# Where the low parts of expert_u are made during a top-16 search: GpSimd from SBUF in place of VectorE from PSUM

## The reference, cut to what matters

```python
q = (xt @ w_pq).reshape(n_tok, 8, 2, 128)
scores = einsum('thcd,hckd->thck', q, sub_keys)      # 256 tokens, 16 sets of 128 scores
s_top, i_top = top_k(scores, 16)                     # for both halves of each of 8 heads
cand = s_top[:, :, 0, :, None] + s_top[:, :, 1, None, :]
best, pos = top_k(cand.reshape(n_tok, 8, 256), 16)
expert_idx = take_along_axis(cand_idx, pos)          # cand_idx = i_top[0]*128 + i_top[1]
gate = softmax(best)
act = gelu(einsum('thkd,td->thk', expert_u[expert_idx], xt))
out = einsum('thk,thkd->td', gate * act, expert_v[expert_idx])
```

## Time and profile before

| | |
|---|---|
| Median of three runs | 2268.61 us (2268.48 to 2272.78) |
| The profiled execution | 2266.69 us |
| its span | 2264.9 us |
| granted TensorE clock, mean | 0.976 |
| busy: PE, DVE, ACT, POOL | 93%, 72%, 49%, 12% of the span |
| first product with expert_u | 616.72 us from the span's start |
| part A | about 617 to 1044 us |
| pairs 26 to 63 | about 1044 to 1540 us |
| products with expert_v, last norm | about 1540 to 2265 us |

### The profile page before, as it was taken

One profiled execution on the slowest core, in us unless ns is written; L12 is line 12 of the kernel. 1 busy time (PEld: TensorE's weight loads), 2 busy tenths in 40 slices (PEclk: granted clock), 3 DMA queues, 4 the chain that ended last, 5 costly groups with the idle time before them and its releaser, 6 DMA issues.

```text
span 2264.9 us, 42561 instructions
## 1 busy us (share of the span) xinstructions
PE 2104.1 (93%) x12326; PEld 1860.0 (82%) x12326; DVE 1631.0 (72%) x2645; ACT 1108.1 (49%) x1888; POOL 270.6 (12%) x171
## 2 busy tenths in 40 slices
PE   8998898979878778889999999999999999999995
PEld 7887786768777777879999999998788888888884
DVE  4556656665588888989999999996555555555556
ACT  4554454445422222334666666655455555555552
POOL 0003301000100000002444444410000000000001
PEclk9999998989999999999999999999999999999998
DMA  7764452647444444545555555566865565555552
GB/s 231 221 207 144 142 169 82 209 144 205 135 125 119 122 112 124 144 139 164 161 157 158 159 157 157 159 174 200 225 202 191 193 193 194 193 192 192 193 194 103
DMA packets 253812, 378.42 MB, mean 167 GB/s; under 512 B 41809, under 2 KB 173009, under 8 KB 253137
## 3 DMA queue, kind: packets, MB, share of 16 engines
q1 hardware_dynamic: 253776, 377.98, 55.7%
HBM read 373.69 MB, written 4.19 MB: 167 GB/s over the span
## 4 chain that ended last, share of the span: by engine, by line
PE 51%; DVE 13%; issue 7%; DVEq 1%; SPq 0%; DMA 0%; ACT 0%; POOL 0%; ACTq 0%
PE ps L406 16%; PE ps L407 16%; PE ps L408 16%; DVE split_lo L1229 5%; PE ps L650 3%; DVE ps L1240 1%; DVE onehot L1397 0%; DVE onehot L1392 0%; DVE head_i L1299 0%; DVE pick_n L1402 0%; SPq L383 0%; DMA raw<-in_expert_v 0%; DVE head_p L1319 0%; DVE head_i L1307 0%; DVE head_p L1316 0%
## 5 line engine op out<-in xcount | busy, mean ns | idle before, releaser
L972 DVE TENSOR_TENSOR split_lo<-raw,split_hi 128x512 fp32r<-128x512 f32 x864 | 623.6, 725 | 519.6 <-ACT split_hi L717 519.4
L717 ACT ACTIVATE split_hi<-raw 128x512 fp32r<-128x512 f32 x864 | 544.4, 631 | 605.8 <-PE ps L408 588.7
L406 PE MATMUL ps<-act_hi,split_hi 128*128 128x256 f32 x2048 | 607.9, 297 | 82.5 <-DVE split_lo L1229 81.6
L407 PE MATMUL ps<-act_lo,split_hi 128*128 128x256 f32 x2048 | 586.5, 286 | 0.0
L408 PE MATMUL ps<-act_hi,split_lo 128*128 128x256 f32 x2048 | 586.0, 286 | 0.0
L876 ACT ACTIVATE split_hi<-ps 128x512 fp32r<-128x512 f32 x512 | 292.6, 594 | 465.3 <-DVE ps L1240 252.6
L406 PEld LDWEIGHTS ps<-act_hi,split_hi 128*128 128x128 f32 x2048 | 399.3, 195 | 107.2 <-DVE split_lo L1229 105.7
L406 PE MATMUL ps<-split_hi,whalf_hi 128*128 128x512 f32 x1024 | 398.7, 389 | 3.2 <-DVE split_lo L972 3.2
L407 PEld LDWEIGHTS ps<-act_lo,split_hi 128*128 128x128 f32 x2048 | 400.6, 196 | 0.0
L408 PEld LDWEIGHTS ps<-act_hi,split_lo 128*128 128x128 f32 x2048 | 399.5, 195 | 0.0
L407 PE MATMUL ps<-split_lo,whalf_hi 128*128 128x512 f32 x1024 | 398.4, 389 | 0.0
(11 more groups left out here) (172 smaller groups left out, 1448.8 us busy)
## 6 DMA issues: line engine op xcount, KB each, us to landing
raw<-in_expert_u SPq DMA_DIRECT2D x1024, 128.0 KB, 2.9
raw<-in_expert_v SPq DMA_DIRECT2D x256, 512.0 KB, 4.6
raw<-in_w_in SPq DMA_DIRECT2D x112, 512.0 KB, 3.8
raw<-in_w_out SPq DMA_DIRECT2D x32, 512.0 KB, 4.1
raw<-in_w_pq SPq DMA_DIRECT2D x128, 128.0 KB, 2.8
cst<-in_tables SPq DMA_DIRECT2D x4, 576.0 KB, 5.1
x_nat<-in_x SPq DMA_DIRECT2D x4, 512.0 KB, 6.9
x_dram<-x_cols SPq DMA_DIRECT2D x1, 2048.0 KB, 7.9
```

The lines of the kernel that those rows point to most:

```text
L406: nc.tensor.matmul(acc, l_hi, r_hi, start=first, stop=False)
L407: nc.tensor.matmul(acc, l_hi, r_lo, start=False, stop=False)
L717: nc.scalar.activation(split_hi[:, q % SPLITS, :], raw[:, q // 2, q % 2, :], ACT.Copy).then_inc(hi_ready, 1)
L972: vec.tensor_tensor(split_lo[:, q % SPLITS, :], raw[:, q // 2, q % 2, :], split_hi[:, q % SPLITS, :].bitcast(f32), ALU.subtract).then_inc( ...
```

## The change

For pairs 0 to 25 the transposes write to a new SBUF buffer, `u_cols` (four halves, 16 KB a partition), in place of PSUM. ScalarE rounds from `u_cols`. GpSimd makes all eight low parts of each of these pairs (208 in all), as a subtraction with both operands and the result in SBUF. VectorE keeps the transposes and the search, in a new order in which a transpose stands between an instruction and the one that needs it. ScalarE copies each set's scores to `head_s` (two buffers now) and keeps the results of each search (three copies), two sets behind and ahead. ScalarE rounds the first four units between the last score evictions, and the first transposes no longer wait for the evictions. The second fill of ones becomes two. From pair 26 on everything is as before. The core of the diff (definitions of buffers, and the removal of the parameters `own`, `part_a`, `nxt`, `next_a`, which had one value each, are left out):

```diff
+        u_cols = at("u_cols", [RAWS, 2, COLS], f32, W0 + 57344)
...
             def split_u(pair, q, part_a):
+                act.wait_ge(dve_turned, turned_at(q // 2, pair))
                 act.wait_ge(split_free, pair * 8 + (Q_U + q + 1))
-                nc.scalar.activation(split_hi[:, q % SPLITS, :], ps[:, 4 + q % 4, :], ACT.Copy).then_inc(hi_ready, 1)
+                src = u_cols[:, q // 2, q % 2, :] if part_a else ps[:, 4 + q % 4, :]
+                nc.scalar.activation(split_hi[:, q % SPLITS, :], src, ACT.Copy).then_inc(hi_ready, 1)
+            def stage_set(n, s):
+                if not isinstance(n, int):
+                    act.wait_ge(ranked, n - 1)
+                nc.scalar.activation(head_s[:, s, :, :], sc3[:, bass.ds(n * 2, 2), :], ACT.Copy
+                                     ).then_inc(set_staged, 1)
+            def keep_set(n, s):
+                act.wait_ge(ranked, n + 1)
+                nc.scalar.activation(idx_f[:, bass.ds(n, 1), :, :].rearrange("p a c k -> p (a c) k"), head_i[:, s, :, :],
+                                     ACT.Copy)
+                nc.scalar.activation(best[:, bass.ds(n, 1), :].rearrange("p a k -> p (a k)"), head_b[:, s, :], ACT.Copy)
+                nc.scalar.activation(pos_u[:, bass.ds(n, 1), :].rearrange("p a k -> p (a k)"), head_p[:, s, :],
+                                     ACT.Copy).then_inc(set_kept, 1)
...
                 for q in range(4, 8):
                     split_u(pair, q, part_a)
                 gelu(pair, 0, 0 in late_tiles)
+                if kept is not None:
+                    keep_set(*kept)
+                if staged_set is not None:
+                    stage_set(*staged_set)
                 split_u(pair + 1, 0, next_a)
...
+            for f in range(8):
+                act.wait_ge(sc_ready, f + 1)
+                nc.scalar.activation(scores[:, f // 4, f % 4 * 4:f % 4 * 4 + 4, :].rearrange("p s k -> p (s k)"),
+                                     ps[:, 2 + f % 2, :], ACT.Copy).then_inc(sc_out, 1)
+                if f == 1:
+                    act.wait_ge(sc_out, 1)
+                    for s in range(2):
+                        stage_set(s, s)
+                if f >= 4:
+                    split_u(0, f - 4, True)
+            u_pair(0, True, True)
+            with act.Fori(0, PH - 1) as i:
+                u_pair(i * 2 + 1, True, True, kept=(i * 2, 0), staged_set=(i * 2 + 2, 0))
+                u_pair(i * 2 + 2, True, True, kept=(i * 2 + 1, 1), staged_set=(i * 2 + 3, 1))
+            u_pair(SOFT - 1, True, True, kept=(SOFT - 2, 0))
+            u_pair(SOFT, True, True, kept=(SOFT - 1, 1))
...
+            def turn_u(pair, k, part_a=False):
+                dve.wait_ge(raw_ready[k], pair * DMA4 + (U_RAW + DMA4))
+                if part_a:
+                    if not (isinstance(pair, int) and pair == 0):
+                        dve.wait_ge(lo_ready, pair * 8 + (Q_U + 2 * k - 6))
+                    dst = u_cols[:, k, :, :]
...
+            def rank_set(lc, n, s):
+                dve.wait_ge(set_staged, n + 1)
+                dve.sem_inc(carried, 1)
+                dve.wait_ge(set_kept, n + 1)
+                dve.sem_inc(carried, 1)
+                turn_u(n + 1, 0, True)
+                top = [lc.add(vec.max(top_v[:, c, 0:8], cols[c])) for c in range(2)]
+                left = []
+                for c in range(2):
+                    lc.until(top[c])
+                    lc.add(vec.max_index(head_i[:, s, c, 0:8], top_v[:, c, 0:8], cols[c]))
+                    left.append(lc.add(vec.match_replace(half_rest[c], top_v[:, c, 0:8], cols[c], LOWEST)))
+                low = []
+                for c in range(2):
+                    lc.until(left[c])
+                    low.append(lc.add(vec.max(top_v[:, c, 8:16], half_rest[c])))
+                turn_u(n + 1, 1, True)
+                lc.until(low[1])
+                sums = lc.add(vec.tensor_tensor(cand[:, :, :], ...))
+                for c in range(2):
+                    lc.add(vec.max_index(head_i[:, s, c, 8:16], top_v[:, c, 8:16], half_rest[c]))
+                lc.until(sums)
+                first = lc.add(vec.max(head_b[:, s, 0:8], pairs))
+                turn_u(n + 1, 2, True)
+                lc.until(first)
+                lc.add(vec.max_index(head_p[:, s, 0:8], head_b[:, s, 0:8], pairs))
+                rest_of = lc.add(vec.match_replace(rest[:, :], head_b[:, s, 0:8], pairs, LOWEST))
+                lc.until(rest_of)
+                second = lc.add(vec.max(head_b[:, s, 8:16], rest[:, :]))
+                turn_u(n + 1, 3, True)
+                lc.until(second)
+                vec.max_index(head_p[:, s, 8:16], head_b[:, s, 8:16], rest[:, :]).then_inc(ranked, 1)
...
+                compared = [compare(h) for h in range(2)]
+                turn_u(pair, 0, True)
+                lc.until(compared[1])
+                selected = [select(h) for h in range(2)]
+                turn_u(pair, 1, True)
+                lc.until(selected[1])
+                collected = [collect(h) for h in range(2)]
+                turn_u(pair, 2, True)
+                turn_u(pair, 3, True)
+                lc.until(collected[1])
...
+                    def split_lo_u(pair, q):
+                        pool.wait_ge(hi_ready, pair * 8 + (Q_U + q + 1))
+                        eng.tensor_tensor(split_lo[:, q % SPLITS, :], u_cols[:, q // 2, q % 2, :],
+                                          split_hi[:, q % SPLITS, :].bitcast(f32), ALU.subtract).then_inc(lo_ready, 1)
+                    for q in range(8):
+                        split_lo_u(0, q)
                     pool.wait_ge(x1_out, 16)
                     pool.wait_ge(sc_ready, 8)
-                    top = 96
-                    eng.memset(wexp[:, LATE:top, :], 1.0).then_inc(ones_ready, 1)
+                    free_rows, kept_rows = 56, 88
+                    eng.memset(wexp[:, LATE:free_rows, :], 1.0).then_inc(ones_ready, 1)
+                    with pool.Fori(1, PAIRS_A) as i:
+                        for q in range(8):
+                            split_lo_u(i, q)
+                    pool.wait_ge(lo_ready, Q_U + 8 * PAIRS_A)
+                    eng.memset(wexp[:, free_rows:kept_rows, :], 1.0)
                     pool.wait_ge(topk_done, 1)
-                    eng.memset(wexp[:, top:NT, :], 1.0).then_inc(ones_ready, 1)
+                    eng.memset(wexp[:, kept_rows:NT, :], 1.0).then_inc(ones_ready, 1)
```

More of the change, by code:

```diff
@@ L244, in fill_place, with turned_at @@
             return f // 2 % 2, (f // 4 * 2 + f % 2) * 4
[L246 to L261, removed]
         PQ_RAW = Q_PQ // 8 * DMA1
         U_RAW = PQ_RAW + (Q_U - Q_PQ) // 8 * DMA4
-        V_RAW = [U_RAW + PAIRS_A * (DMA4 if k in DVE_A else DMA1)
-                 + (PAIRS - PAIRS_A) * (DMA4 if k in DVE_B else DMA1) for k in range(RAWS)]
+        V_RAW = U_RAW + PAIRS * DMA4
+        def turned_at(half, pair):
+            return pair * RAWS + (half + 1)
         block = ctx.enter_context(nc.Block())
@@ L614, in _, with score_pair @@
                 last.then_inc(sc_ready, 1)
-            def score_pair(pair, own, part_a, nxt=None, next_a=False, after=None):
+            def score_pair(pair, after=None):
                 for q in range(8):
@@ L1264, in add, with until @@
                     instruction.then_inc(v_chain, 1)
-                def step(self, instruction):
-                    self.add(instruction)
-                    dve.wait_ge(v_chain, self.i * self.steps + (self.first + self.n))
+                    return self.n
+                def until(self, n):
+                    dve.wait_ge(v_chain, self.i * self.steps + (self.first + n))
                     dve.sem_inc(carried, 1)
@@ L1333, in late_tile @@
+            with dve.Fori(0, PH) as i:
+                lc = LoopChain(i, c0, TOP_STEPS)
+                for s in range(2):
+                    rank_set(lc, i * 2 + s, s)
+                assert lc.n == TOP_STEPS, lc.n
+            chain.n += PH * TOP_STEPS
             def late_tile(pair, t):
@@ L1346, in apply_gates, with u_pair @@
                                   ).then_inc(gates_free, 1)
-            def u_pair(pair, own, part_a, nxt, next_a, late_tiles=False, groups=None, between=None):
+            def u_pair(pair, groups=None, between=None):
                 for k in (2, 3):
-                    split_turn(pair, k, own, part_a, nxt, next_a)
-                    if late_tiles and k == 2:
-                        if groups is not None and not isinstance(groups, int):
+                    split_turn(pair, k)
+                    if k == 2:
+                        if groups is not None:
                             dve.wait_ge(gates_free, groups + 2)
@@ L1358, in u_pair @@
                 for k in (4, 5):
-                    split_turn(pair, k, own, part_a, nxt, next_a)
-                    if late_tiles and k == 4:
+                    split_turn(pair, k)
+                    if k == 4:
                         if groups is not None:
```

(10 more changed lines are left out.)

193 lines of the change are left out of this document (65 added, 128 removed).

## The result

The changed kernel takes 2141.32 us (median of four runs, 2139.91 to 2144.47); the kernel before took 2268.55 beside it. The ratio is 0.9428, 95% interval 0.9415 to 0.9441. The forecast was 2141 us, 2134 to 2188. A second set of runs of the same file, `after_again`, the baseline of the experiments, gave 2140.72 us (five runs, 2140.44 to 2142.16), ratio 0.9431 (0.9417 to 0.9444).

What follows compares the result with a forecast made beforehand. VectorE's program order bounded part A, then TensorE would: start 613.8 plus 300.9 us gives 914.7 against 1044.1, 129.4 less, minus 2 for jams; 2266.69 - 127.4 = 2139.3, median 1.9 higher: 2141 us, range 2134 to 2188.

Steps and rivals of the forecast that it cites:

- TensorE the bound of part A, full clock, pitch 0.12: Pairs 0 to 25: TensorE always busy at full clock, 0.12 us a matmul, 11.52 us a pair; chance 62%.
- GpSimd's low part, 1.08 us: Each of GpSimd's 208 subtractions of 128x512 was to take 1.08 us, 8.6 us a pair against 11.52.
- The numbering on GpSimd, 11.0 of 11.52: In a numbering pair GpSimd needs 8.6 us for low parts plus 2.4 held by VectorE, 11.0 of TensorE's 11.52.
- second rival: GpSimd becomes the bound at 1.75 us a low part, 14.0 a pair: 64 us lost, 2205 us; chance 11%.
- The shared way into SBUF: VectorE's two-input instructions wait for GpSimd's running one: `cand` 0.4 us, four a numbering pair 0.7 each, holding GpSimd 0.6.
- Pair 16 on VectorE, about 7 us: In pair 16 VectorE has four transposes and the start of the softmax, about 7 us against 11.5, winning slack back.
- VectorE, a search, 10.9: VectorE's work in one search falls from 17.56 us to 10.9 (10.3 to 11.6), or 11.3 with port waits.
- first rival: VectorE stays the bound, 13.0 us a search and 14.2 a numbering: 33 us lost, 2174 us; chance 18%.
- ScalarE: ScalarE's added staging and keeping copies bring it to at most 7.4 of 11.52 us a search, costed at nothing.
- The start: Part A's first product comes at 613.8 us against 616.72, 2.9 us earlier, from 0 to 3.7.
- The end of part A: Two GpSimd fills of ones, 15.6 us, stay hidden behind pairs 25 and 26 by 1 us or more.
- The sum: Whole forecast: 26 pairs at 11.52, 1.4 for slow matmuls, earlier start, 2 us for jams: 127.4 us saved.

Runs made afterwards that it cites:

- pool_kinds: Changed kernel plus six GpSimd subtractions and products of 128x512 alone at its very start, with two full operands or one repeated; 2146.59 us (single run).
- exposed: Changed kernel with VectorE waiting for its own result before its transposes, not behind them, at three places of a search; 2140.55 us, ratio 0.9423.

## Why the prediction was right, point by point

- **TensorE the bound of part A, full clock, pitch 0.12:** as forecast. Measured to the same point as before (0.6 us ahead of the gelu, 1044.1 there and 921.5 here), part A took 921.5 - 618.73 = 302.8 us; the prediction had 300.9 and 2 for jams.
- **GpSimd's low part, 1.08 us: wrong,** 1.30 alone and 1.37 as the mean of all 208. The step that failed is "1.75 is about 1.1 plus one 0.6 of VectorE, so I take 1.08": all the rows of 1.04 to 1.12 had a repeated operand, which I had noted and then not priced, and `pool_kinds` puts the second full operand at 0.22. The row of 1.75 was read wrongly with it: like the low parts that meet VectorE (1.74 to 1.79) it fits 1.3 and a hold of 0.46, not 1.1 and 0.6. A row with two full operands was in the trace before, the 2.56 us for 1024 columns shown under `pool_kinds`; it gives 1.28. The Trainium skill's factor of about two (GPSIMD Engine Reference, "When to use GPSIMD") gave an estimate of 1.38, and I set it aside because of those rows; it was the nearer of the two (1.30 / 0.68 = 1.9). What saved the sum is the room: 281 us of work in 299.9 rather than 249 in 299.5.
- **The numbering on GpSimd, 11.0 of 11.52: wrong in both terms,** which partly cancel. Back to back, low parts that meet nothing start 1.26 us apart (a little less than they last, as they overlap), so eight are 10.1; the iteration is 11.93, so each of the four two-input instructions of VectorE holds GpSimd for (11.93 - 10.1) / 4 = 0.46, not 0.6. It ends 0.4 over TensorE's pace. Eight times that is 3.3, and TensorE lost 2.8 in 797 to 914 us. The second rival was therefore true for eight pairs of 26, at a price of 3 us instead of 15.
- **The shared way into SBUF:** right in kind, small in the sum. `cand` takes 0.38 when free and 1.04 to 1.52 when it waits, 0.54 on the mean: 0.16 of wait where I took 0.4. The comparisons and products wait 0.64 and 0.40 on the mean (1.325 and 1.076 against 0.68) where I took 0.7; singly they take 0.64 to 0.97 or 1.45 to 1.79. Transposes take 1.19 to 1.25 beside a busy GpSimd, and sums 0.65. The Trainium skill's rule (SBUF — State Buffer, "Who interferes with whom"), that VectorE instructions with one SBUF input go free outside the two-port modes and those with two do not, agrees with all of these.
- **Pair 16 on VectorE, about 7 us: a missed term.** I gave the softmax's start (a copy, a subtraction of two operands, two operations with a constant and a conversion) no wait, though the earlier trace rows shows a copy that waited. All five waited, two of them here:

```profile
814.33 1.38 DVE L1371 TENSOR_SCALAR pos_i<-pos_u 128x256 uint32<-128x256 uint32 x1
...
817.09 1.48 DVE L1373 CAST pos_f<-pos_i 128x512 f32<-128x512 uint32 x1
```

  In the kernel before, with GpSimd idle, these two took 0.29 and 0.43 us. The start of the softmax took 6.2 us (812.4 to 818.6), so with four transposes 10.9. That is still under 11.52.
- **VectorE, a search, 10.9:** lower. One period, with the row's wait taken off:

```profile
631.24 1.25 DVE L1249 STREAM_TRANSPOSE u_cols<-raw 128x1024 f32<-128x1024 f32 x1 [1.21 <-POOL split_lo L1575]
...
641.47 1.25 DVE L1249 STREAM_TRANSPOSE u_cols<-raw 128x1024 f32<-128x1024 f32 x1
```

  Work without a wait for GpSimd takes 641.47 - 631.24 = 10.23 us, its `cand` of 1.06 included, under the lower end of my 10.3 to 11.6 plus port wait. The order hid nearly all the stalls, and `exposed` shows that it need not have. The first rival (VectorE the bound, 18%) was 1.3 us a search away, and in the numbering VectorE was idle 1.27 us an iteration (10.66 us of work where I took 12.2); two more two-input instructions were enough to bring it about.
- **ScalarE:** costed at nothing, and that held; staging and keeping took 0.20 to 0.41 each, behind no wait.
- **The start:** 2.9 us forecast, 3.7 measured (16.19 from `q_t` to the first product before, 12.53 after), and the allowance of 1.4 for slow matmuls was not needed, as TensorE came without a gap.
- **The end of part A:** as forecast. The fills took 15.6 us (6.94 and 8.65) and ended 4.3 us before GpSimd's next work had its input:

```profile
917.97 6.94 POOL L1588 MEMSET wexp<- 128x8192 f32 x1
924.85 8.65 POOL L1590 MEMSET wexp<- 128x10240 f32 x1
937.76 3.76 POOL L1597 TENSOR_TENSOR hot<-small,picks_t 128x1024 f32<-128x1024 f32 x2 [4.26 <-DVE picks_t L1438]
```

- **The sum:** 127.4 forecast for the stretch, 128.3 measured: the start brought 0.8 more than forecast, and part A 0.1 (302.8 against 302.9). That part A came out so close is partly luck: the 1.4 us for slow matmuls were not needed, and the loss in the numbering was larger than the 2 us for jams. That GpSimd's 0.22 a piece stayed off the path is not luck but room, which the prediction had worked out too large.

## What to carry to other kernels

Before moving work to an engine, price it by a row with the same kind of operands, not only the same size; here there was one, in another part of the same trace. If there is none, take the pessimistic figure and see what still fits (here the verdict survived an error of a fifth only because the new bound had that much room). Look at the tightest stretch and not at the mean, and count matmuls, not only busy time. A careful order can be worth much on the bounding engine and nothing one change later, so undo each part alone to see which still pays. And look at single instructions before reading a mean: a row that merges two can hide that one waits and the other doesn't.

## What the runs showed of the hardware

- On GpSimd a 128x512 f32 subtraction with two full operands takes 1.30 us, and a product with one operand repeated 1.08 (a product of 1024 columns with two full ones took 2.56 in the kernel before); an fp32r result adds nothing.
- A VectorE instruction with two SBUF operands of 128x512 waits until GpSimd's running subtraction ends (up to 1.79 us in all against 0.68), and holds GpSimd's next for some 0.46 us in return (1.74 to 1.79 against 1.30). Where they met six times in 13.59 us, VectorE looked busy for 75.0 of 75 us and GpSimd for 71.2.
- Copies, conversions and operations with a constant on VectorE, SBUF to SBUF, can wait for GpSimd too. Of four small copies in a row one or two did (means 0.42, 0.17, 0.31 and 0.61 us against 0.18, 0.16, 0.16 and 0.28); in the softmax's start all of them did (1.30 to 1.48 us against 0.29 to 0.43 for the 128x256 and 128x512 ones).
- TensorE's first matmuls ran at a pitch of 0.12 us where it had no gap before them (granted clock 1.00), and of 0.22 behind a gap of 4.59 us (granted clock 0.50 for the first 3 us, 1.00 within 4.5 us).
